# Attention phase: the order of GpSimd's late-modulation pieces and the place of their eviction

## The chip, the cores and the metric

The kernel runs on one core of a Trainium2 chip. The metric is the device time of one execution in microseconds (us). The time before is the median of three runs.

## What is computed

One layer of a hybrid diffusion model over 2048 latent tokens of width 1024 with 256 context tokens: a modulation, a mixer (a recurrent group and a windowed attention group), an output projection with a layer norm and a second modulation, and a mixture of experts. Cut to what matters here:

```
m_lat = silu_c @ w_mod[l] + b_mod[l]
sh1, sc1, g1, sh2, sc2, g2 = jnp.split(m_lat[:, None, :], 6, axis=-1)
h_lat = modulate(x, sh1, sc1)
# window_attention: scores over a band of 3*128 keys and 256 context keys, with a sink
p = jax.nn.softmax(jnp.concatenate([s_band, s_ctx, s_sink], -1), axis=-1)
# after the mixer
x = layer_norm(ALPHA * x + g1 * y_lat, ln1_g[l], ln1_b[l])
h_lat = modulate(x, sh2, sc2).reshape(B * S, D)
```

The second half of m_lat (sh2, sc2, g2; 3072 columns) isn't needed before the output projection. The kernel computes it beside attention: this is the "late modulation".

## The kernel before

The program is a row of phases, each a block in which every engine has its own instruction stream, and the next phase begins when all streams of the block have ended.

**Attention** (phase_attention) goes over 16 tiles of 128 queries, in 8 pairs (PAIRS), each tile with 8 heads (NH). For a head, TensorE makes the scores (L1099), VectorE takes the row minimum of the negated scores (L1157), ScalarE the exponent with its sum (L1190), TensorE transposes it (L1111), ScalarE copies the high half (L1199), VectorE makes the low half (L1163), and TensorE multiplies with the values (L1128 to L1130). The order is written out by hand in `pairs`; the first pair and the last stand outside the loop. Once in a tile comes the sink: GpSimd's `inverse` subtracts (L1045), ScalarE takes the exponent (exp_sink, L1207, between the exponent of head 7 and the copy of head 6), GpSimd adds (L1050) and inverts (L1055), and VectorE's `normalise` (L1175) scales the tile's result, which SP stores (L1021).

Between the inverses GpSimd works off two other things:
- The late modulation: for each of 8 slabs of w_mod (128 rows of 3072 columns, 1.5 MB), three pieces of 1024 columns: a multiplication with a column of c (L1069) and an addition to `late` (L1071). SP loads slabs 0 and 1 (L1013, `load_late`) behind w_out, its companions and a row of b_mod (L1008), and each further one when the pieces of the slab that it overwrites are done. The first piece of a slab waits for its load.
- A row of w_out is multiplied with g1 (L1080), once in a pair, and at the end gnc is scaled (L1081).

**Output** (phase_output): TensorE first sums `late` over the partitions into PSUM (L1596). ScalarE evicts these sums (L1517), SP stores them as rows (L1301), waits, and loads sh2 and sc2 back as broadcasts (L1304); VectorE adds 1 to sc2 (L1462) within its step for tile 0. ScalarE then makes the high halves of the 8 blocks of w_out (`high_w`, L1476), four before the first tile's `prepare` (L1482 to L1497) and four behind it; VectorE makes the low halves (L1368). TensorE's products of a tile need them. VectorE's long chain of the layer norm begins at L1401.

Of the kernel before, what the change touches and what calls it, by code (L numbers as in the profile page):

```python
# [12 lines left out]
ALU = mybir.AluOpType  # L13
ACT = mybir.ActivationFunctionType
# [3 lines left out]
D = 1024  # L18
KD = D // P
# [164 lines left out]
LATE_N = LATE_W // 8  # L184


def late_modulation(arena):

    return arena[:, 0:LATE_W]


OUT_W0 = 27000
# [722 lines left out]
def phase_attention(nc, env):  # L915
# [3 lines left out]
    g = env  # L919
    sem, arena, ps, ps_row, small, idn = g["sem"], g["arena"], g["ps"], g["ps_row"], g["small"], g["idn"]  # L920
# [17 lines left out]
    late_ld, late_ok, late_d = g["done"]["wmod_ld"][0:2], g["done"]["wmod_ld"][3], g["done"]["win_hi"]  # L938
    LATE_LD, LATE_OK, LATE_D = DONE["wmod_ld"], DONE["wmod_ld"], DONE["win_hi"]
    late = late_modulation(arena)  # L940
    slab = [arena[:, LATE_W * (j + 1):LATE_W * (j + 2)] for j in range(2)]
    assert 3 * LATE_W <= KT0
    LATE_P = LATE_W // D
# [4 lines left out]
    PAIRS = T_LAT // 2  # L948
# [39 lines left out]
    with nc.Block() as block:  # L988
# [47 lines left out]
        @block.gpsimd  # L1036
        def _(pool):

            def inverse(i, j):
                t = 2 * i + j  # L1040
                pool.wait_ge(s_min, START + NH * t + NH)
                pool.sem_inc(g["alone"], 1)
                pool.wait_ge(es_e, START + t)
                pool.sem_inc(g["alone"], 1)
                nc.gpsimd.tensor_tensor(es[j], nm[j], neg_sink, ALU.subtract).then_inc(es_d, 1)  # L1045
                pool.wait_ge(es_e, START + t + 1)
                pool.sem_inc(g["alone"], 1)
                pool.wait_ge(p_d, START + NH * t + NH)
                pool.sem_inc(g["alone"], 1)
                nc.gpsimd.tensor_tensor(es[j], den[j], es[j], ALU.add).then_inc(den_d, 1)  # L1050
                pool.wait_ge(den_d, START + 2 * t + 1)
                pool.sem_inc(g["alone"], 1)
                pool.wait_ge(o_d, START + t)
                pool.sem_inc(g["alone"], 1)
                nc.gpsimd.tensor_tensor(rd[j], es[j], minus, ALU.pow).then_inc(den_d, 1)  # L1055

            nc.gpsimd.memset(minus, -1.0).then_inc(w_gate, 1)
            pool.wait_ge(neg_ok, START + 1)
            pool.wait_ge(w_gate, START + 1)
            nc.gpsimd.memset(late, 0.0).then_inc(late_ok, 1)  # L1060

            def late_terms(k, lo, hi):
                if lo == 0:
                    pool.wait_ge(late_ld[k % 2], LATE_LD + 16 * (k // 2) + 16)
                    pool.wait_ge(late_ok, LATE_OK + 17)
                for n in range(lo, hi):
                    at = LATE_D + 2 * (LATE_P * k + n)
                    cols = slice(n * D, (n + 1) * D)
                    nc.gpsimd.tensor_scalar(slab[k % 2][:, cols], slab[k % 2][:, cols], g["c_col"][:, k:k + 1], None, ALU.mult)                        .then_inc(late_d, 1)  # L1069
                    pool.wait_ge(late_d, at + 1)  # L1070
                    nc.gpsimd.tensor_tensor(late[:, cols], late[:, cols], slab[k % 2][:, cols], ALU.add).then_inc(late_d, 1)  # L1071
            for i in range(PAIRS):
                inverse(i, 0)
                late_terms(i, 0, 2)
                inverse(i, 1)
                late_terms(i, 2, LATE_P)

                pool.wait_ge(w_ld, START + 16 * 7)
                row = arena[:, OUT_W0 + i * D:OUT_W0 + (i + 1) * D]
                nc.gpsimd.tensor_tensor(row, row, ow["g1"], ALU.mult).then_inc(w_gate, 1)  # L1080
            nc.gpsimd.tensor_scalar(ow["gnc"], ow["gnc"], W_SCALE, None, ALU.mult).then_inc(w_gate, 1)  # L1081

        @block.tensor
# [127 lines left out]
def phase_output(nc, env):  # L1211
# [3 lines left out]
    g = env  # L1215
    sem, arena, ps, ps_row, small, idn = g["sem"], g["arena"], g["ps"], g["ps_row"], g["small"], g["idn"]
    late = late_modulation(arena)
# [6 lines left out]
    late_rows = b["late_rows"].rearrange("p (i n) -> p i n", i=2)  # L1224
    late_mm, late_ev, late_st, late_ld = (g["done"][name] for name in ("mod_mm", "rows_done", "rows_st", "win_ld"))
    LATE_MM, LATE_EV, LATE_ST, LATE_LD = (DONE[name] for name in ("mod_mm", "rows_done", "rows_st", "win_ld"))
# [15 lines left out]
    sq, hi, lo, ssm, ss_d, ssv_d, pw_s = (sem("e_sq"), sem("e_hi"), sem("e_lo"), sem("e_ssm"), sem("e_ss"), sem("e_ssv"),  # L1242
                                              sem("e_pw_s"))
# [8 lines left out]
    def tiles(eng, first, step, finish):  # L1252

        first()
        step(0, 0)
        step(1, 1)
        with eng.Fori(1, T_LAT // 2 - 1) as i:
            step(2 * i, 0)
            step(2 * i + 1, 1)
        step(T_LAT - 2, 0)  # L1260
        step(T_LAT - 1, 1)
        finish()

    def known(t, low):

        return not isinstance(t, int) or t >= low

    def has_next(t):

        return not isinstance(t, int) or t + 1 < T_LAT  # L1270

    def half(t):

        return t // 2 if isinstance(t, int) else t >> 1
    with nc.Block() as block:
# [197 lines left out]
        @block.scalar  # L1473
        def _(act):
            def high_w(k):
                nc.scalar.activation(whi[:, k, :], wo[:, k, :], ACT.Copy, scale=b["gnc"][:, k:k + 1]).then_inc(w_hi, 1)  # L1476

            def prepare(t, j):
                act.wait_ge(in_ld[j], START + 32 * half(t) + 32)

                act.wait_ge(fold_d, START + 2 * t)
                nc.scalar.activation(b["ysq"], b[f"yT{j}"], ACT.Square).then_inc(sq, 1)  # L1482

                if known(t, 2):
                    act.wait_ge(o_y, START + t - 1)
                nc.scalar.activation(yhi[j], b[f"yT{j}"], ACT.Copy, scale=X_SCALE).then_inc(hi, 1)

                if known(t, 2):
                    act.wait_ge(ssv_d, START + t - 1)
                act.wait_ge(sq, START + 2 * t + 1)  # L1490
                nc.scalar.activation(b["asq"], b[f"at{j}"], ACT.Square, accum_out=ss[j][:, 1:2]).then_inc(sq, 1)
                act.wait_ge(a_tr, START + t + 1)
                if known(t, 2):
                    act.wait_ge(o_mm, START + t - 1)
                nc.scalar.activation(ahi[j], ps[:, 6, :], ACT.Copy, scale=X_SCALE).then_inc(hi, 1)
                act.wait_ge(ssm, START + t + 1)
                nc.scalar.activation(ss[j][:, 0:1], ps[:, 7, 64:65], ACT.Copy).then_inc(ss_d, 1)  # L1497

            def scaled(t, j):
                act.wait_ge(o_y, START + t + 1)  # L1500
                act.wait_ge(pw_s, START + t + 1)

                if known(t, 1):
                    act.wait_ge(v, START + NV * t - NV + 1)
                nc.scalar.activation(b["t0"], ps_row[:, 1024:2048], ACT.Copy, scale=sr[j][:, 0:1]).then_inc(o_act, 1)

            def route(t):
                for n in range(2):
                    act.wait_ge(h_tr, START + 2 * t + n + 1)

                    if n == 0:
                        act.wait_ge(r_mm, START + t)
                    nc.scalar.activation(b["h2T"][:, n * 512:(n + 1) * 512], ps[:, n, :], ACT.Copy).then_inc(h_ev, 1)

            def first():
                act.wait_ge(late_mm, LATE_MM + 1)
                nc.scalar.activation(late_rows, ps[:, 0:2, 0:LATE_N], ACT.Copy).then_inc(late_ev, 1)  # L1517
                for k in range(C_RNN):
                    high_w(k)
                prepare(0, 0)  # L1520
                for k in range(C_RNN, KD):
                    high_w(k)

            def step(t, j):
                if has_next(t):
                    prepare(t + 1, 1 - j)
                if known(t, 2):
                    route(t - 2)
                scaled(t, j)

            def finish():
                route(T_LAT - 2)
                route(T_LAT - 1)
            tiles(act, first, step, finish)

        @block.tensor
# [879 lines left out]
```

## Time and profile before

| | us |
|---|---|
| median of three runs | 2130.78 |
| lowest, highest | 2127.84, 2132.82 |
| profiled execution, its time | 2130.82 |
| its span, first to last instruction | 2129.0 |
| attention, from SP's first instruction to that of the output phase | 576.68 to 827.17 |

Times in the rows further down count from the start of this span. The name of an engine stands with the line of the kernel: L1207 ACT is the exponent of the sink. PE is TensorE, DVE VectorE, ACT ScalarE, POOL GpSimd, and SPq the DMA issues of SyncE. In a timeline each row has start, duration, engine, line and operation, and in brackets how long the engine sat idle before it and what ended this.

### The profile page before, as it was taken

To read this page: it belongs to the slowest core of one execution; us is meant where nothing else is said; L and a number is where in the kernel's file an instruction comes from. 1 tells how busy PE (TensorE), PEld (TensorE's weight loads), DVE (VectorE), ACT (ScalarE), POOL (GpSimd) and SP (SyncE) were. 2 spreads that over 40 slices of the span, in tenths; PEclk is the share of its full clock that TensorE was granted. 3 is DMA by queue.
4 is the path that set the end of the run, shared out by engine and by line. 5 is a ranking of instruction groups with operands and counts; after the bars stand their busy time and mean duration, and the time that the engine had idled before them with its cause. 6 is when DMAs were issued, how large, how long until landed. Compare 5 with 4: busy or idle time off the path is not lost. (4 is left out here: it accounts for less than half of the span.)

```text
span 2129.0 us, 41055 instructions
## 1 busy us (share of the span) xinstructions
PE 1782.7 (84%) x11690; PEld 1022.7 (48%) x11693; DVE 1496.2 (70%) x1855; ACT 1039.1 (49%) x1362; POOL 553.7 (26%) x456
## 2 busy tenths in 40 slices
PE   3488989799389996999914999999999889899947
PEld 0366666344177774555512454544444444444412
DVE  2576666488689996888978345666769888755537
ACT  2234243677378886333204134445556666534326
POOL 0000000000057785333313121223324323222213
PEclk9799999999799998999956999999999999999979
DMA  9321220565563322344336357886979999887537
GB/s 377 90 90 60 89 79 36 200 220 180 181 228 119 116 90 90 119 158 141 136 109 236 112 155 216 289 295 205 364 242 374 374 377 372 295 276 222 181 82 274
DMA packets 167790, 417.62 MB, mean 196 GB/s; under 512 B 16233, under 2 KB 24881, under 8 KB 166065
## 3 DMA queue, kind: packets, MB, share of 16 engines
q1 hardware_dynamic: 152898, 362.85, 46.8%
q0 software_dynamic: 14832, 54.01, 10.4%
q8 instruction: 33, 0.54, 0.1%
q14 instruction: 27, 0.22, 0.0%
HBM read 343.38 MB, written 73.44 MB: 196 GB/s over the span
## 5 line engine op out<-in xcount | busy, mean ns | idle before, releaser
L2060 DVE SCALAR_TENSOR_TENSOR arena<-arena 128x2048 f32 (+1 forms) x186 | 421.3, 2289 | 108.1 <-ACT arena L2004 50.9
L2140 PE MATMUL ps<-arena 128*128 x1200 | 458.3, 382 | 44.0 <-DVE arena L2060 43.8
L2141 PE MATMUL ps<-arena 128*128 x1200 | 458.1, 382 | 0.0
L2142 PE MATMUL ps<-arena 128*128 x1200 | 457.9, 382 | 0.0
L1998 ACT ACTIVATE arena<-arena 128x2048 f32 (+1 forms) x124 | 233.2, 1908 | 149.5 <-DMA arena<-w 62.3
L640 PE MATMUL ps<-arena 128*128 128x256 f16 (+1 forms) x1680 | 235.1, 301 | 21.1 <-DVE arena L525 21.1
L2140 PEld LDWEIGHTS ps<-arena 128*128 128x128 f16 x1200 | 118.0, 98 | 185.3 <-issue 59.0
L640 PEld LDWEIGHTS ps<-arena 128*128 128x128 f16 x1680 | 164.7, 99 | 85.7 <-DVE arena L525 15.2
L2142 PEld LDWEIGHTS ps<-arena 128*128 128x128 f16 x1200 | 118.1, 98 | 139.8 <-issue 3.4
L2141 PEld LDWEIGHTS ps<-arena 128*128 128x128 f16 x1200 | 117.9, 98 | 131.6 <-issue 3.5
L2004 ACT ACTIVATE arena<-arena 128x2048 f32 (+1 forms) x62 | 117.4, 1908 | 69.1 <-DMA arena<-w 52.6
L2060 DVE SCALAR_TENSOR_TENSOR arena<-ps,arena 128x512 f16<-128x512 f32 (+1 forms) x101 | 96.5, 955 | 68.9 <-ACT arena L2021 42.6
L1157 DVE CUSTOM_DVE_ANT_0 arena<-ps,arena,small 128x640 f32<-128x640 f32 x128 | 112.8, 881 | 16.5 <-issue 7.0
L1964 POOL COPY ix<-gidx 128x1 int32 (+1 forms) x50 | 26.0, 519 | 364.2 <-DVE arena L2097 364.2
L1099 PE MATMUL ps<-arena 128*128 (+3 forms) x768 | 93.0, 258 | 31.6 <-DMA arena<-qT_d 30.4
L2011 ACT ACTIVATE arena<-ps 128x1024 f16<-128x1024 f32 x51 | 52.0, 1020 | 122.8 <-PE ps L2135 122.8
L1111 PE MATMUL ps<-idn,arena 128*128 128x128 f32 x640 | 93.2, 276 | 20.5 <-ACT arena L1190 9.7
L1199 ACT ACTIVATE arena<-ps 128x640 f16<-128x640 f32 x128 | 90.1, 704 | 37.9 <-PE ps L1130 32.5
L1190 ACT ACTIVATE arena<-arena,small 128x640 f32<-128x640 f32 x128 | 105.0, 820 | 6.1 <-DVE small L1157 6.1
L1163 DVE SCALAR_TENSOR_TENSOR arena<-ps,arena 128x640 f16<-128x640 f32 x128 | 104.9, 819 | 3.1 <-ACT arena L1199 3.1
L2097 DVE SCALAR_TENSOR_TENSOR arena<-ps,gslot,arena 128x1024 f32<-128x1024 f32 x50 | 64.0, 1280 | 60.9 <-PE ps L2142 45.6
L1968 POOL DMA_INDIRECT x_d<-arena,ix x50 | 94.7, 1893 | 42.3 <-POOL ix L1964 38.5
(296 smaller groups left out, 3272.8 us busy)
## 6 DMA issues: line engine op xcount, KB each, us to landing
arena<-w SPq DMA_DIRECT2D x186, 1024.0 KB, 12.1
arena<-hT_d SPq DMA_DIRECT2D x64, 512.0 KB, 6.0
arena<-w_mod SPq DMA_DIRECT2D x16, 1536.0 KB, 8.0
h_d<-arena SPq DMA_DIRECT2D x17, 512.0 KB, 3.0
x_d<-arena SPq DMA_DIRECT2D x17, 512.0 KB, 2.6
arena<-x SPq DMA_DIRECT2D x8, 1024.0 KB, 6.4
hT_d<-arena SPq DMA_DIRECT2D x16, 512.0 KB, 3.1
arena<-x SPq DMA_DIRECT2D x16, 512.0 KB, 4.8
```

The lines of the kernel that those rows point to most:

```text
L640: mm = pe.matmul(o, lhs, rhs, start=first and n == 0, stop=last and n == 2)
L1111: mm = pe.transpose(pT(m)[:, q * P:(q + 1) * P], b[f"s{m % 4}"][:, q * P:(q + 1) * P], idn[:])
L1157: nc.vector.tensor_tensor_reduce(b[f"s{m % 4}"], scores_at(m), b[f"mask{j}"], -undo, neg_sink[:, h:h + 1], ALU.add, ALU.min, nm[j][:, h:h ...
L1163: nc.vector.scalar_tensor_tensor(b[f"plo{m % 2}"].bitcast(F16), pT(m), P_SCALE, b[f"phi{m % 2}"].bitcast(F16), ALU.mult, ALU.subtract).the ...
L1190: nc.scalar.activation(b[f"s{m % 4}"], b[f"s{m % 4}"], ACT.Exp, bias=nm[j][:, h:h + 1], scale=-1.0, accum_out=den[j][:, h:h + 1]).then_inc ...
L1968: pool.indirect_dma_start(g["x1_d"], bass.IndirectOffsetOnAxis(ix[:, 2:3], 0), b["y0"], None, compute_op=ALU.add)\
L1998: nc.scalar.activation(part(buf, whi, n * PIECE, PIECE), b["st"][:, n * PIECE:(n + 1) * PIECE], ACT.Copy, scale=W_SCALE).then_inc(hi13, 1)
L2004: nc.scalar.activation(part(buf, whi, n * PIECE, PIECE), b["st"][:, n * PIECE:(n + 1) * PIECE], ACT.Copy, scale=W_SCALE).then_inc(hi2, 1)
L2060: return nc.vector.scalar_tensor_tensor(dst, src, scale, high, ALU.mult, ALU.subtract)
L2140: pe.matmul(out, high, part(buf, whi, at, 512), start=first, stop=False)
L2141: pe.matmul(out, high, part(buf, wlo, at, 512), start=False, stop=False)
L2142: return pe.matmul(out, low, part(buf, whi, at, 512), start=False, stop=last)
```

## The change

GpSimd's stream in attention is put in another order. Before, for pair i: inverse of the even tile, pieces 0 and 1 of slab i, inverse of the odd tile, piece 2, gated row. After: pieces 0 and 1 of slab i, inverse of the even tile, piece 2, gated row, inverse of the odd tile. The scaling of gnc stays last. In the output phase, ScalarE's wait for TensorE's sums and their eviction move from the front of its stream to behind the first four `high_w` and the first tile's `prepare`. SP's, VectorE's and TensorE's streams aren't edited.

```diff
-            def late_terms(k, lo, hi):
-                if lo == 0:
+            def late_term(k, n):
+                if n == 0:
                     pool.wait_ge(late_ld[k % 2], LATE_LD + 16 * (k // 2) + 16)
                     pool.wait_ge(late_ok, LATE_OK + 17)
...
-            for i in range(PAIRS):
-                inverse(i, 0)
-                late_terms(i, 0, 2)
-                inverse(i, 1)
-                late_terms(i, 2, LATE_P)
+            def gated_row(k):
 
                 pool.wait_ge(w_ld, START + 16 * 7)
-                row = arena[:, OUT_W0 + i * D:OUT_W0 + (i + 1) * D]
+                row = arena[:, OUT_W0 + k * D:OUT_W0 + (k + 1) * D]
                 nc.gpsimd.tensor_tensor(row, row, ow["g1"], ALU.mult).then_inc(w_gate, 1)
+            for k in range(KD):
+                late_term(k, 0)
+                late_term(k, 1)
+                inverse(k, 0)
+                late_term(k, 2)
+                gated_row(k)
+                inverse(k, 1)
...
             def first():
-                act.wait_ge(late_mm, LATE_MM + 1)
-                nc.scalar.activation(late_rows, ps[:, 0:2, 0:LATE_N], ACT.Copy).then_inc(late_ev, 1)
                 for k in range(C_RNN):
                     high_w(k)
                 prepare(0, 0)
+                act.wait_ge(late_mm, LATE_MM + 1)
+                nc.scalar.activation(late_rows, ps[:, 0:2, 0:LATE_N], ACT.Copy).then_inc(late_ev, 1)
                 for k in range(C_RNN, KD):
                     high_w(k)
```

## Rows read from the trace of the kernel before

**Rows 1.** Busy time by stretch, middle of attention (columns named)
```profile
core 0: us, PE busy (x) PEld busy (x) DVE busy (x) ACT busy (x) POOL busy (x), PEclk, DMA share, GB/s
640.00:800.00 160.00, 146.58 (x2304) 124.66 (x2301) 149.07 (x277) 134.75 (x277) 121.47 (x72) 1.00 0.31 108
```

**Rows 2.** Groups by line, GpSimd: busy us, mean ns, then idle before
```profile
L1069 POOL TENSOR_SCALAR arena<-arena,c_col 128x1024 f32<-128x1024 f32 x24 | 68.4, 2852 | 5.0 <-DMA arena<-w_mod 5.0
```

**Rows 3.** Timeline of GpSimd, first and second tile of attention
```profile
603.78 2.86 POOL L1069 TENSOR_SCALAR arena<-arena,c_col 128x1024 f32<-128x1024 f32 x1 [5.05 <-DMA arena<-w_mod]
...
614.32 0.20 POOL L1045 TENSOR_TENSOR small<-small 128x8 f32<-128x8 f32 x1
```

**Rows 4.** Timeline of ScalarE: the sink's exponent of tiles 0, 1
```profile
596.14 0.20 ACT L1207 ACTIVATE small<-small 128x8 f32<-128x8 f32 x1
...
614.55 0.21 ACT L1207 ACTIVATE small<-small 128x8 f32<-128x8 f32 x1 [1.72 <-POOL small L1045]
```

**Rows 5.** Timeline of SP: the first two slabs of w_mod
```profile
594.10 2.26 SPq L1013 DMA_DIRECT2D arena<-w_mod  x2
```

**Rows 6.** Timeline of SP: mask loads at the ends of tiles 2, 3, 13
```profile
627.23 0.33 SPq L995 DMA_DIRECT2D arena<-masks  x1
...
641.51 0.33 SPq L995 DMA_DIRECT2D arena<-masks  x1
...
786.24 0.33 SPq L995 DMA_DIRECT2D arena<-masks  x1
```

**Rows 7.** Waits of 560 to 630 (us, times, longest), then those of L1157
```profile
PE ps L1099 <- DMA arena<-qT_d: 30.4, 2, 28.0
...
  POOL small L1045: 0.8, 5
```

**Rows 8.** Timeline of GpSimd and SP, end of attention; the store's landing time
```profile
815.50 0.21 POOL L1045 TENSOR_TENSOR small<-small 128x8 f32<-128x8 f32 x1
...
826.61 0.24 POOL L1081 TENSOR_SCALAR arena<-arena 128x8 f32<-128x8 f32 x1
821.14 0.32 SPq L1021 DMA_DIRECT2D attn_d<-arena  x1
827.17 0.37 SPq L1279 DMA_DIRECT2D arena<-yT_d  x1
...
DMA to landing us min/median/max: 2.0/2.0/2.0
```

**Rows 9.** Timeline, start of the output phase; landing of mod_rows' transfers
```profile
830.24 0.81 ACT L1517 ACTIVATE arena<-ps 128x768 f32<-128x768 f32 x1 [11.51 <-PE ps L1596]
830.95 4.25 ACT L1476 ACTIVATE arena<-arena 128x1024 f16<-128x1024 f32 x4
...
839.57 4.25 ACT L1476 ACTIVATE arena<-arena 128x1024 f16<-128x1024 f32 x4
...
831.08 2.46 SPq L1301 DMA_DIRECT2D mod_rows<-arena  x4
835.20 0.81 SPq L1304 DMA_DIRECT2D arena<-mod_rows  x2
...
DMA to landing us min/median/max: 4.0/4.9/15.1
...
846.73 0.68 DVE L1462 TENSOR_SCALAR arena<-arena 128x1024 f32<-128x1024 f32 x1
...
854.78 1.28 DVE L1401 SCALAR_TENSOR_TENSOR arena<-ps,small,arena 128x1024 f32<-128x1024 f32 x1 [6.14 <-PE ps L1569]
```

**Rows 10.** Busy time by stretch: TensorE's start and its pause
```profile
580.00:584.00 4.00, 2.81 (x16) 1.81 (x17) 0.89 (x2) 0.52 (x1) 1.16 (x1) 0.50 1.00 313
584.00:588.00 4.00, 3.26 (x29) 2.31 (x28) 2.89 (x7) 3.00 (x8) 0.00 (x0) 0.97 1.00 402
...
821.00:822.00 1.00, 0.00 (x0) 0.00 (x0) 0.05 (x1) 0.00 (x0) 0.92 (x1) 1.00 0.04 14
...
824.00:825.00 1.00, 0.00 (x0) 0.00 (x0) 0.00 (x0) 0.00 (x0) 1.00 (x2) 0.50 0.00 0
```

More of the change, by code:

```diff
@@ L1060, in _ @@
             nc.gpsimd.memset(late, 0.0).then_inc(late_ok, 1)
-            def late_terms(k, lo, hi):
-                if lo == 0:
+            def late_term(k, n):
+                if n == 0:
                     pool.wait_ge(late_ld[k % 2], LATE_LD + 16 * (k // 2) + 16)
                     pool.wait_ge(late_ok, LATE_OK + 17)
[L1066 to L1071, printed above, removed]
-            for i in range(PAIRS):
-                inverse(i, 0)
-                late_terms(i, 0, 2)
-                inverse(i, 1)
-                late_terms(i, 2, LATE_P)
+                at = LATE_D + 2 * (LATE_P * k + n)
+                cols = slice(n * D, (n + 1) * D)
+                nc.gpsimd.tensor_scalar(slab[k % 2][:, cols], slab[k % 2][:, cols], g["c_col"][:, k:k + 1], None, ALU.mult)\
+                    .then_inc(late_d, 1)
+                pool.wait_ge(late_d, at + 1)
+                nc.gpsimd.tensor_tensor(late[:, cols], late[:, cols], slab[k % 2][:, cols], ALU.add).then_inc(late_d, 1)
+            def gated_row(k):
                 pool.wait_ge(w_ld, START + 16 * 7)
-                row = arena[:, OUT_W0 + i * D:OUT_W0 + (i + 1) * D]
+                row = arena[:, OUT_W0 + k * D:OUT_W0 + (k + 1) * D]
                 nc.gpsimd.tensor_tensor(row, row, ow["g1"], ALU.mult).then_inc(w_gate, 1)
+            for k in range(KD):
[5 more added lines that the diff above has]
+                inverse(k, 1)
             nc.gpsimd.tensor_scalar(ow["gnc"], ow["gnc"], W_SCALE, None, ALU.mult).then_inc(w_gate, 1)
```

## The prediction

> **What bounds the kernel now.** I read the table of busy time by stretch first, over the middle of attention. In 160 us VectorE is busy for 149.07, TensorE for 146.58, ScalarE for 134.75 and GpSimd for 121.47 [rows 1]. So the attention loop is paced by the chain score, exponent, transpose, copy, low half, product, which runs through three nearly full engines. GpSimd isn't full. It is only a side branch, but one which ScalarE must wait for once in a tile: exp_sink (L1207) needs the subtraction at L1045, and ScalarE takes its instructions in order. While it stands there no further exponent and no further copy of a transposed tile is made, and so VectorE and TensorE stop after one or two more heads.
>
> Next I read the timeline of the two places that the change touches: the first tile and the border to the output phase. One piece of the late modulation is a multiplication (2852 ns on the mean [rows 2]) and a somewhat shorter addition on GpSimd. In the timeline two pieces last 614.32 - 603.78 = 10.54 us [rows 3].
>
> **Part 1: two pieces in front of the first tile.** In the kernel before, ScalarE's exp_sink of tile 0 ran at 596.14, without a wait [rows 4]. GpSimd began the first piece only at 603.78, after an idle stretch that the arrival of the first w_mod slab ended [rows 3]: SP had issued this load at 594.10 [rows 5], behind w_out, the broadcasts and the b_mod row. Nothing of the change touches that queue before this point, and GpSimd's instructions before it are the same too. So the slab lands at 603.78 again. But now GpSimd waits for it, and adds the two pieces, before the first inverse. The subtraction for tile 0 then starts at 614.32, which is just where before it started for tile 1 [rows 3], and exp_sink of tile 0 runs at 614.55 instead of 596.14: ScalarE is held for 18.41 us. That is the added wait. Behind it on ScalarE are the copy of head 6 and all exponents from head 8 on, and behind these VectorE's low halves, TensorE's products, and SP's store of tile 0.
>
> Not all of that is lost. In the kernel before, tile 1 was slow: its exp_sink also stood until 614.55, because GpSimd had started its two pieces late [rows 4], and TensorE's second wait for a q load was 30.4 - 28.0 = 2.4 us there [rows 7]. After the change that load is long in when ScalarE is released. So tile 1 after is released at 614.55, in the same way as tile 2 was before, and its minima should be complete where those of tile 2 were, at about 627.23; SP's mask loads mark these moments [rows 6]. Tile 2 after comes one odd-to-even step later. From the end of tile 3 to that of tile 13 are five pairs of tiles, (786.24 - 641.51) / 5 = 28.95 us each, and the even-to-odd step in a pair is 641.51 - 627.23 = 14.28 [rows 6], so the odd-to-even step is 14.67. From then on everything is one tile step late: **+14.7 us**. Bounds: 14.3 (the shorter step) below, and 18.4 above (if none of tile 1's slowness is given back).
>
> **Part 2: TensorE's clock.** In the stall TensorE has no work for some 16 us. The trace shows what that does: with TensorE idle at the end of attention, the granted clock was 1.00 at 821 to 822 and 0.50 (1.2 GHz) at 824 to 825 [rows 10]. When TensorE had begun attention it stood at 0.50 at 580 to 584, with 2.81 us of work, and at 0.97 on average at 584 to 588 [rows 10]. So the release at 614.55 restarts at 1.2 GHz for about 3.4 us. With TensorE over 91% busy in the loop [rows 1], half of that is lost: **+1.7 us**, an estimate. Bounds: 0 (the chain hides it) and 2.3 (4.6 us at the low clock, if the pauses between the heads keep it low longer). The Trainium skill, page "TensorE: Matmul & The Clock Gate", section "HAM oscillation — how this bites in real kernels", says the same of waits for data: the cold penalty is half of the throttled time. It speaks against this change, which opens such a pause; by a sum without this rule the forecast would be 1.7 lower.
>
> **Part 3: the steady loop.** The order in GpSimd's stream alternates as before (two pieces, inverse, one piece with a gated row, inverse), only the two pieces now stand in the odd-to-even gap, the longer one (14.67 against 14.28). In the kernel before, the last odd inverse started at 815.50 with no idle time in front of it [rows 8], about 1 us after the minima were there. But hardly anyone waited: VectorE's L1157 waited for it 0.8 us in all, in 5 places [rows 7]. I take **0**; bounds -0.8 and +0.5. SP's refill of a slab (L1013) waits for pieces that are now done earlier, so it is issued some us sooner, behind the store of the odd tile, in a stretch in which the DMA queues are mostly empty: 0.
>
> **Part 4: the end of attention.** In the kernel before, SP issued the last store at 821.14, which takes 2.0 us to land, so 823.1. The next phase began at 827.17 [rows 8], since GpSimd still had a piece, a gated row and the scaling of gnc (826.61 [rows 8]). After the change only the scaling is left behind the last inverse; it is done before the store. What is last now is the store: the phase begins at about 823.1 + 0.4 = 823.5 of the old time scale. **-3.7 us**; bounds -3.9 and -3.3.
>
> **Part 5: the eviction of the sums.** Before, ScalarE's first step in the output phase (the copy at L1517) waited for TensorE's sums until 830.24, and high_w began at 830.95 [rows 9], 3.78 us after the phase began at 827.17 [rows 8]. Now high_w starts at once, and everything up to the first tile's sums comes about 3.75 sooner. The first tile's loads don't stop that: they are issued in the same order, and ScalarE wants them only after four high_w of 4.25 us together [rows 9]. Then the copy stands in front of the second four high_w; its place in the line is 830.95 - 830.24 = 0.71. So high_w(4), 839.57 before [rows 9], comes 3.75 - 0.71 = **3.0 us** sooner, and with it TensorE's products and VectorE's first long chain (854.78 [rows 9]). Bounds: 0 and -3.75.
>
> What is late next: the rows. SP's four row stores, their wait and the two broadcasts stand behind the copy. Before, the stores were issued at 831.08, the broadcasts at 835.20 [rows 9], 4.1 later. After (in the old scale of the phase) the copy ends at about 836.6, the broadcasts are issued near 840.8 and land a median of 4.9 us later [rows 9], near 846. VectorE wants them at L1462, 846.73 before [rows 9], so 843.7 now: it stands for some 2.5 us. It has nothing on the path there until 854.78 - 3.0 = 851.8. That is its cover: 0. The refill for tile 2 (L1279 in SP's queue) stands behind the broadcasts too and now waits with them, to about 842. ScalarE wants it behind the second high_w (839.57 + 4.25 - 3.0 = 840.8) and the whole prepare of tile 1, which needs sums from GpSimd and TensorE; I count that as some 6 us more, near 847, and the refill as landed by then. Also 0, with little to spare.
>
> **The sum**, against the profiled execution (span 2129.0, its time 2130.82, practically the median of 2130.78): +14.7 + 1.7 + 0 - 3.7 - 3.0 = **+9.7 us**, so **2140.5 us**, slower by 0.45%. The phases behind (route, experts, combine) read what the output phase leaves and shift as a whole.
>
> **The rivals.**
> First, *the output phase gives nothing back*: the late rows or tile 2's refill hold VectorE or ScalarE long enough to eat part 5. Price 3.0: +12.7, 2143.5. It decides if the rows land after about 851. For it: two more queues now hang on the copy. Against it: 5 us of cover.
> Second, *the loop runs faster*: the lateness of GpSimd on odd tiles (about 1 us in each of 7 pairs) is on the path after all, and goes. Price -7: +2.7, 2133.5, within 0.2%. Against it: the 0.8 us of rows 7.
> Third, on the other side, *no stall at the first tile*: the wait that I see as 18.41 us would be covered, parts 1 and 2 fall away, and 4 and 5 remain: -6.7, 2124.1. It decides where slab 0 lands before 596.14 - 0.2 - 10.5 = 585.4, so that both pieces are done when exp_sink comes. For it: the end of attention is really freed. Against it: SP issues the load only at 594.10 [rows 5]. The change as a whole turns faster if the shift in attention is under 6.7 us.
>
> **How the numbers follow.** The forecast has 78 in 100, the first rival 10, the second 7, the third 5. A difference of 0.2% (4.3 us) is about what a measurement of this kernel can tell from no change; the three runs before spread from 2127.84 to 2132.82. Of the forecast's 78 I count 2 as ending within 0.2%. So slower 86, same 9, faster 5. The terms' bounds, not all at one end at once, and half of the spread of the runs give 2135.5 to 2144.5; this takes in the first rival, and leaves out the other two.
>
> **What will show it.** L1207's first wait: some 18 us on GpSimd's L1045 at 614.5 (part 1). SP's mask load for the second tile near 627 to 629, and 28.9 us for each pair from there. The granted clock at 0.50 around 614 to 618 (part 2). The output phase's first load about 0.4 us behind the landing of the last store (part 4), L1476 in its first tenth of a microsecond, and L1401's first start 24.6 us after the phase begins, against 854.78 - 827.17 = 27.6 before (part 5). Wrong it would be made by a slab that lands at another time, or by the cold restart being longer than one head or two.

## The result and the profile after

The changed kernel takes 2143.41 us (median of six runs, 2137.03 to 2145.09), against 2130.89 for the kernel before (six runs, 2127.84 to 2133.57): a ratio of 1.0056, 95% interval 1.004 to 1.0071. It is slower, by 12.5 us on the medians and 11.9 by the ratio (the ratio isn't simply that of the two medians, so the two readings differ a little in each run below). Measured again in another series (label a2_change_again, below) the ratio was 1.0039, interval 1.0027 to 1.0051, so 8.3 us, or 9.1 on the medians. The forecast was +9.7.

The profiled execution of the changed kernel has a span of 2135.2 us. Its attention begins at 577.18, 0.50 later than before (576.68), which is subtracted where positions are compared below. What changed lines are called now: the sink's exponent is L1211, the first late piece L1068, high_w L1480, the eviction L1524, VectorE's first long chain L1405.

First the timeline of ScalarE and of GpSimd at the first tiles; the rows of before that answer to them are [rows 3] and [rows 4].

```profile
596.32 0.82 ACT L1194 ACTIVATE arena<-arena,small 128x640 f32<-128x640 f32 x1
...
615.02 0.21 ACT L1211 ACTIVATE small<-small 128x8 f32<-128x8 f32 x1 [17.79 <-POOL small L1045]
...
630.79 0.20 ACT L1211 ACTIVATE small<-small 128x8 f32<-128x8 f32 x1
```

```profile
604.30 2.85 POOL L1068 TENSOR_SCALAR arena<-arena,c_col 128x1024 f32<-128x1024 f32 x1 [22.68 <-DMA arena<-w_mod]
607.24 2.34 POOL L1071 TENSOR_TENSOR arena<-arena 128x1024 f32<-128x1024 f32 x1
609.56 2.84 POOL L1068 TENSOR_SCALAR arena<-arena,c_col 128x1024 f32<-128x1024 f32 x1
612.48 2.34 POOL L1071 TENSOR_TENSOR arena<-arena 128x1024 f32<-128x1024 f32 x1
614.78 0.21 POOL L1045 TENSOR_TENSOR small<-small 128x8 f32<-128x8 f32 x1
```

ScalarE's last exponent of tile 0 begins at 596.32, and the sink's exponent at 615.02: 17.79 us of waiting for L1045. GpSimd's rows say where they come from. The slab lands at 604.30, 7.1 us after ScalarE became ready, and the two pieces last 10.5 us. In the whole attention this is the only wait of L1211.

Then TensorE in the stall, in the table of busy time by stretch (after the stretch: its length, busy time and count of PE, PEld, DVE, ACT and POOL, the granted clock, DMA share, GB/s). Before, all of these stretches stood at 1.00.

```profile
600.00:604.00 4.00, 0.00 (x0) 0.00 (x0) 0.00 (x0) 0.00 (x0) 0.00 (x0) 1.00 1.02 430
604.00:608.00 4.00, 0.00 (x0) 0.00 (x0) 0.00 (x0) 0.00 (x0) 3.62 (x2) 0.53 0.70 280
...
616.00:618.00 2.00, 1.18 (x7) 1.15 (x8) 2.00 (x4) 2.00 (x5) 2.00 (x2) 0.50 0.03 8
618.00:620.00 2.00, 2.00 (x24) 1.81 (x23) 0.90 (x2) 1.01 (x3) 2.00 (x1) 0.50 0.04 8
620.00:622.00 2.00, 2.00 (x26) 1.76 (x25) 0.44 (x3) 0.77 (x3) 1.92 (x2) 0.67 0.00 0
622.00:624.00 2.00, 0.88 (x11) 0.69 (x10) 2.00 (x5) 1.27 (x3) 2.00 (x2) 1.00 0.30 120
```

The clock falls to 0.50 while TensorE has nothing to do, and the first work behind the stall, from 616.8 to about 621.3, runs at the low clock, 1.2 GHz.

SP's mask loads mark the ends of tiles 1, 2, 3 and 13, the counterparts of [rows 6]:

```profile
629.04 0.33 SPq L995 DMA_DIRECT2D arena<-masks  x1
...
644.10 0.33 SPq L995 DMA_DIRECT2D arena<-masks  x1
...
658.50 0.33 SPq L995 DMA_DIRECT2D arena<-masks  x1
...
803.07 0.33 SPq L995 DMA_DIRECT2D arena<-masks  x1
```

Tile 1 now ends at 629.04, where before tile 2 ended at 627.23. A pair takes (803.07 - 658.50) / 5 = 28.91 us, against 28.95 before: the steady loop is untouched.

Last the border and the start of the output phase, on SP, ScalarE and VectorE, against [rows 8] and [rows 9]:

```profile
825.04 13.24 SPq L1021 DMA_DIRECT2D attn_d<-arena  x2
840.45 0.37 SPq L1283 DMA_DIRECT2D arena<-yT_d  x1
...
849.92 2.46 SPq L1305 DMA_DIRECT2D mod_rows<-arena  x4
853.49 0.81 SPq L1308 DMA_DIRECT2D arena<-mod_rows  x2
```

```profile
840.47 4.26 ACT L1480 ACTIVATE arena<-arena 128x1024 f16<-128x1024 f32 x4 [4.92 <-PEq L988]
...
849.09 0.81 ACT L1524 ACTIVATE arena<-ps 128x768 f32<-128x768 f32 x1
849.78 4.26 ACT L1480 ACTIVATE arena<-arena 128x1024 f16<-128x1024 f32 x4
...
860.73 0.63 ACT L1486 ACTIVATE arena<-arena 128x512 f32<-128x512 f32 x1 [0.16 <-DMA arena<-attn_d]
```

```profile
859.18 0.69 DVE L1466 TENSOR_SCALAR arena<-arena 128x1024 f32<-128x1024 f32 x1 [2.13 <-DMA arena<-mod_rows]
...
864.71 1.28 DVE L1405 SCALAR_TENSOR_TENSOR arena<-ps,small,arena 128x1024 f32<-128x1024 f32 x1 [4.64 <-PE ps L1573]
```

The last store is issued at 825.04 + 13.24 - 0.32 = 837.96, and the next phase begins 2.5 us later. High_w begins with the phase. VectorE stands for 2.13 us for the broadcasts, and then still 4.64 us for TensorE. Its first long chain starts 24.26 us behind the phase's start, against 27.61 before.

### The profile page after: what moved, and what is told of

Its sections match the earlier page's. It is cut to its first block and busy times, and to the rows that moved or that the text cites. A ratio compares the mean times of both kernels' runs of the same rounds, so it can differ in the third digit from the quotient of the medians.

```text
span 2135.2 us, 41055 instructions
## 1 busy us (share of the span) xinstructions
PE 1788.0 (84%) x11690; PEld 1025.5 (48%) x11693; DVE 1495.1 (70%) x1855; ACT 1039.2 (49%) x1362; POOL 550.7 (26%) x456
## 3 DMA queue, kind: packets, MB, share of 16 engines
q0 software_dynamic: 14832, 54.01, 10.4%
```

## The experiments

The time of a whole execution spreads by several microseconds even with the same kernel. The experts phase alone, which no edit touches, took 922.5 to 929.2 us in the traces (925.4 in the kernel before, 922.5 in the changed one). So besides the ratio each experiment is read by three stretches of its trace, with SP's first instruction of a phase as mark: *attention*; *start*, from the output phase's first instruction to VectorE's first long chain; and *both*, from attention's first instruction to the end of the output phase.

| kernel | ratio to before (95%) | attention | start | both |
|---|---|---|---|---|
| before | | 250.49 | 27.61 | 504.09 |
| the change | 1.0056 (1.004 to 1.0071) | 263.27 | 24.26 | 513.48 |
| a2_change_again | 1.0039 (1.0027 to 1.0051) | 262.27 | 24.27 | 512.53 |
| e1_order_alone | 1.0046 (1.0032 to 1.006) | 262.84 | 27.61 | 516.41 |
| e2_evict_alone | 0.998 (0.9969 to 0.9991) | 252.41 | 24.27 | 502.64 |
| e7_one_piece | 1.0012 (1.0 to 1.0023) | 258.61 | 24.27 | 508.83 |
| e6b_keep_warm_65 | 1.0035 (1.0025 to 1.0045) | 260.16 | 24.28 | 510.41 |
| e6_keep_warm | 1.0084 (1.007 to 1.0098) | 270.95 | 24.26 | 521.16 |
| e3_tail_only | 0.9969 (0.9958 to 0.998) | 246.26 | 25.96 | 498.19 |
| e4_gap0_light | 0.9951 (0.9936 to 0.9965) | 245.12 | 24.26 | 495.32 |
| e9_early_alone | 0.9991 (0.9981 to 1.0002) | 248.80 | 27.61 | 502.38 |
| e5_slab_early | 0.9949 (0.9935 to 0.9963) | 245.26 | 24.27 | 495.47 |
| e5b_slab_early_again | 0.9952 (0.9936 to 0.9968) | 244.93 | 25.95 | 496.81 |
| e8_tail_and_early | 0.9949 (0.9934 to 0.9963) | 244.15 | 25.95 | 496.04 |

**The two parts, each alone.** e1 takes the changed kernel and puts the eviction back; e2 takes the kernel before and moves the eviction alone.

```diff
 e1, against the changed kernel (e2: the other way round, against the kernel before)
             def first():
+                act.wait_ge(late_mm, LATE_MM + 1)
+                nc.scalar.activation(late_rows, ps[:, 0:2, 0:LATE_N], ACT.Copy).then_inc(late_ev, 1)
                 for k in range(C_RNN):
                     high_w(k)
                 prepare(0, 0)
-                act.wait_ge(late_mm, LATE_MM + 1)
-                nc.scalar.activation(late_rows, ps[:, 0:2, 0:LATE_N], ACT.Copy).then_inc(late_ev, 1)
```

> GpSimd's new order alone, the eviction stays at the front of ScalarE's stream. Theory A (stall at tile 0 of 18 us, of which one tile step and a cold restart stay, minus a free end of attention; the eviction is a term of its own): +14.7 + 1.7 - 3.7 = +12.7 us against before, so about 2143.5. The output phase begins about 12.8 us later than before and VectorE's first long chain again 27.6 us after it. Rival B (the two edits only pay together, since the eviction waits for sums that now come at once): the eviction at the front would cost nothing, so this kernel would be at the time of the full change, +9.4 in the trace up to the end of the output phase.

Measured: attention 12.35 us longer than before, start 27.61 to the hundredth, both +12.3. The eviction is a term of its own, as theory A has it, and rival B falls by the stretch: with the copy in front, the start takes 3.35 us more than in the change. The ratios can't show that: 1.0046 lies between the two measurements of the change.

> The eviction's move alone, GpSimd's order as before. Theory A: -3.0 to -3.4 us (first long chain of VectorE 24.3 us after the phase's start, against 27.6), so about 2127.6; attention unchanged, its last wait still GpSimd's tail. Rival C (the output phase gives it back behind the late rows): 0, 2130.9, with VectorE's first long chain again 27.6 us after the start or a longer wait later in the phase.

Measured: the start is 3.34 us shorter, and the ratio of 0.998 (-4.3 us, interval -6.6 to -1.9) is clear of 1. Rival C falls. Attention itself, with no edit in it, was 1.9 us longer than in the trace of before. Tile 1 did it: the sinks' exponents of tiles 0 and 1 stood at 600.14 and 618.43, 18.3 apart, nearly as before, but those of tiles 1 and 2 were 15.4 apart where before they were 14.1. So a single trace can differ by 1.9 us in attention with no edit there, and differences of that size between two traces, further down, prove little by themselves.

**The change again.**

> The changed kernel itself, once more, timed beside the kernel before on this chip. Theory A says +9.4 us to +9.8 (the shift of the marks up to the end of the output phase), so what the first measurement showed beyond that, +12.5, was spread between executions of the experts phase. Rival F says that about 3 us of it belong to the change, and come back here: +12.5.

Measured: 1.0039, and the stretch *both* +8.4 us. The interval, 5.8 to 10.9 us, leaves 12.5 out. Rival F falls: the 12.5 of the first measurement held some 3 us of spread.

**One piece in front of tile 0.** This measures what a microsecond of stall costs.

```diff
-            for k in range(KD):
-                late_term(k, 0)
-                late_term(k, 1)
-                inverse(k, 0)
-                late_term(k, 2)
-                gated_row(k)
-                inverse(k, 1)
+            late_term(0, 0)
+            pieces = iter([(k, n) for k in range(KD) for n in range(LATE_P)][1:])
+            rows = iter(range(KD))
+            for t in range(T_LAT):
+                inverse(t // 2, t % 2)
+                for _ in range([2, 2, 1, 2, 1, 2, 1, 2, 1, 2, 1, 2, 1, 2, 1, 0][t]):
+                    late_term(*next(pieces))
+                for _ in range([0, 0, 1, 0, 1, 0, 1, 0, 1, 0, 1, 0, 1, 0, 2, 0][t]):
+                    gated_row(next(rows))
```

> The change with one piece in place of two in front of tile 0; the second goes to the gap behind it, the gated rows to odd places further on. Theory A: the wait of the first sink's exponent falls by one piece, 5.3 us, to about 12.5, and all of it shows at the end: -5.3 against the change. With no piece there, the wait for the slab itself (7.7 of the 17.8 us) would go too. Rival H (a stall is given back in the loop, which has slack): the same end of attention as in the change.

The sink's exponent of tile 0, timeline of ScalarE in e7:

```profile
610.46 0.21 ACT L1213 ACTIVATE small<-small 128x8 f32<-128x8 f32 x1 [12.92 <-POOL small L1045]
626.43 0.19 ACT L1213 ACTIVATE small<-small 128x8 f32<-128x8 f32 x1
```

The wait fell from 17.79 (18.08 in the repeated trace) to 12.92, attention by 4.7 and 3.7 us against the two traces of the change, and the median beside a2 from 2141.92 to 2136.77, by 5.2. The stall is passed on about one to one; rival H falls.

**TensorE kept at work in the stall.** This takes away the cold restart (the first work behind the stall at the low clock) alone. The products go to a place in PSUM that is written anew later. e6b has 65 of them in place of 125.

```diff
             def transposes(i, m):
                 n = i * HEADS + m
+                if isinstance(n, int) and n == NH:
+                    for _ in range(125):
+                        pe.matmul(ps[:, 7, 384:512], idn[:], idn[:], start=True, stop=True)
```

> The full change, with 125 products of the identity on TensorE (into the place in PSUM of heads 6 and 7, which are written later) where it would stand idle in the stall of tile 0. Theory A: the granted clock stays at 1.00 through the stall, tile 1 ends 1.3 to 1.7 us sooner than in the changed kernel, total -1.5 against it. Rival E (the cold restart costs nothing on the path, tile 1's extra comes from the restart's latency): no gain in tile 1's end.

It ran into something else: each of these products is two passes of 0.112 us, so the stuffing lasted 28.1 us in place of the 14 that were meant, and TensorE itself became late (timeline of TensorE in e6):

```profile
600.50 28.08 PE L1112 MATMUL ps<-idn 128*128 128x128 f32 x250
628.41 0.71 PE L1119 MATMUL ps<-idn,arena 128*128 128x128 f32 x5
```

It says nothing on the clock's price. e6b has the right size.

> As e6_keep_warm with 65 products in place of 125. In e6 the 250 passes took 28.1 us and outlasted the stall by 12 us, which was not meant; 130 passes take 14.6 us and end about 1.5 us ahead of ScalarE's release. Theory A: clock 1.00 all through, tile 1 (from the first sink's exponent to the second) in about 14.1 us where the change needed 15.8, so -1.7 against the change. Rival E (the cold restart is off the path): 15.8 again.

Timeline of ScalarE in e6b, and one row of its busy time by stretch:

```profile
614.77 0.21 ACT L1215 ACTIVATE small<-small 128x8 f32<-128x8 f32 x1 [16.62 <-POOL small L1045]
628.41 0.20 ACT L1215 ACTIVATE small<-small 128x8 f32<-128x8 f32 x1
```

```profile
616.00:618.00 2.00, 1.43 (x25) 1.43 (x26) 1.96 (x4) 1.94 (x6) 2.00 (x2) 1.00 0.06 16
```

The clock stays at 1.00 all through the stall. The same five transposes are TensorE's first work behind it in both kernels (timeline of TensorE, first the change, then e6b):

```profile
616.82 1.30 PE L1115 MATMUL ps<-idn,arena 128*128 128x128 f32 x5 [17.41 <-DVE arena L1167]
```

```profile
616.57 0.74 PE L1119 MATMUL ps<-idn,arena 128*128 128x128 f32 x5 [1.73 <-DVE arena L1171]
```

From the first sink's exponent to the second it takes 13.64 us. The change took 15.77, its repetition 14.96 (611.98 to 626.94), e1 15.33 (611.84 to 627.17). So the cold restart costs 1.3 to 2.1 us, 1.7 on the mean of three, and rival E falls. The other traces agree: e7, which restarts at 0.50 too, took 15.97, and e5 and e5b (below), whose clock stays at 1.00 behind a short stall, took 13.80 each. In the whole time it can't be told apart: 2141.37 against 2141.92 for a2.

**The free end without the stall.** e3 leaves the front of tile 0 alone and spreads the pieces so that nothing lies behind the last inverse. e4 also makes the first gap light.

```diff
 the loop over k of the changed kernel becomes
+            pieces = iter([(k, n) for k in range(KD) for n in range(LATE_P)])
+            rows = iter(range(KD))
+            for t in range(T_LAT):
+                inverse(t // 2, t % 2)
+                for _ in range(ROWS[t]):
+                    gated_row(next(rows))
+                for _ in range(PIECES[t]):
+                    late_term(*next(pieces))
 e3: PIECES = [2, 1] * 6 + [2, 2, 2, 0];     ROWS = [0, 1] * 4 + [0, 2, 0, 2] + [0] * 4
 e4: PIECES = [1, 2] + [2, 1] * 5 + [2, 2, 2, 0]
     ROWS = [2, 0, 0, 2, 0, 1, 0, 1, 0, 1, 0, 1, 0, 0, 0, 0]
```

> The eviction moved as in the change, but nothing in front of tile 0: GpSimd's gaps 0 to 11 hold 2, 1, 2, 1, ... pieces as in the kernel before, gaps 12 to 14 two each, gap 15 (behind the last inverse) none, the gated rows in the odd gaps up to 11. Theory A: the stall was the price of moving the two pieces to the front, and the free end doesn't need it: -3.7 - 3.3 = -7.0 us against before, 2124; no wait over 3 us of the sink's exponent. Rival G (the loop had no room for the extra pieces: gaps of 10.5 us beside an inverse of 3.9 in a step of 14.3 to 14.7): waits of the sink's exponent in tiles 12 to 15, and more than 2128.

Measured: 0.9969, 6.6 us faster by the ratio and 5.2 on the medians, where 7.0 was expected; attention 4.2 us shorter, and no wait of the sink's exponent but the 2.18 us of tile 1 that the kernel before has too. So rival G falls. The start took 25.96 in place of 24.3, which is told in the last section.

> As e3_tail_only, but the gap behind tile 0 holds two gated rows and one piece in place of two pieces, so that GpSimd is done with them before tile 1 ends although the slab lands late. Theory A: the wait of tile 1's sink (2.2 us in e3) is gone, about -1 to -2 against e3, near -8 against before; the query load that comes late behind the slabs stays. Rival K (that wait was hidden behind the query load anyway): the same as e3.

The timeline of GpSimd and of ScalarE in e4:

```profile
603.51 4.68 POOL L1077 TENSOR_TENSOR arena<-arena 128x1024 f32<-128x1024 f32 x2
608.27 2.85 POOL L1068 TENSOR_SCALAR arena<-arena,c_col 128x1024 f32<-128x1024 f32 x1
```

```profile
600.95 0.20 ACT L1212 ACTIVATE small<-small 128x8 f32<-128x8 f32 x1
...
615.56 0.20 ACT L1212 ACTIVATE small<-small 128x8 f32<-128x8 f32 x1
```

GpSimd fills the time until the slab lands with gated rows, whose data are there. Tile 1's sink doesn't wait any more. The two exponents are 14.6 us apart (18.4 before), of which 1.4 is only that the first came later behind the start of attention; the second came 2.4 us sooner. The ratio is 0.9951: 10.4 us faster than before by the ratio, 8.8 on the medians and by the stretch. Rival K says that this is the same as e3. That isn't settled: attention is 1.1 us shorter than in e3, less than the 1.9 by which e2's trace differed without an edit, and the intervals of the two ratios overlap.

**The slab earlier.** e5 is the full change with another order in SP's queue. e9 is the kernel before with that order alone, e8 is e3 with it.

```diff
             for j in range(2):
                 load(0, j)
 
+            sp.dma_start(slab[0], g["w_mod"][0:P, FRONT:6 * D]).then_inc(late_ld[0], 16)
+            sp.wait_ge(late_ok, LATE_OK + 1)
+            sp.dma_start(late[0:1, :], g["b_mod"][0:1, FRONT:6 * D]).then_inc(late_ok, 16)
             sp.dma_start(wo, g["w_out"].rearrange("(k p) n -> p k n", p=P)).then_inc(w_ld, 16)
...
-            sp.wait_ge(late_ok, LATE_OK + 1)
-            sp.dma_start(late[0:1, :], g["b_mod"][0:1, FRONT:6 * D]).then_inc(late_ok, 16)
...
-            for k in range(2):
-                load_late(k)
+            load_late(1)
```

> The full change, but SP loads slab 0 and the row of b_mod in front of w_out instead of behind it (and slab 1 alone where both stood). Theory A (the stall is the wait for slab 0 plus two pieces, nothing else): the slab lands near 585, both pieces are done near 595.5 to 597, the wait of the first sink's exponent falls from 17.8 us to 0 to 2, the clock stays high, and the whole is -3.7 (free end) - 3.3 (eviction) and up to 3 us of tile 1's slowness before: 2121 to 2125. Rival D (two pieces in front of the inverse hold the first tile by themselves, or the queries of tile 0 come late behind the slab, or w_out comes late for the gated row): more than 5 us of stall stay somewhere in the first two tiles, over 2128.

The timeline of GpSimd and of ScalarE in e5:

```profile
589.19 2.86 POOL L1067 TENSOR_SCALAR arena<-arena,c_col 128x1024 f32<-128x1024 f32 x1 [6.61 <-DMA arena<-b_mod]
```

```profile
599.95 0.21 ACT L1210 ACTIVATE small<-small 128x8 f32<-128x8 f32 x1 [1.22 <-POOL small L1044]
613.75 0.20 ACT L1210 ACTIVATE small<-small 128x8 f32<-128x8 f32 x1
```

The stall shrank to 1.22 us (1.91 in e5b), although both pieces still stand in front of tile 0, and a kernel that was slower by 0.4% to 0.6% became faster by 0.5%. The moment of landing was what decided; rival D falls. The load that GpSimd waited for last was now the row of b_mod, which e5 moves together with the slab, so the two loads aren't told apart. The repetition gave the same (0.9952).

> e5_slab_early once more, so that the three others have it beside them on the same chip: -10 us against before (its marks gave -8.6 up to the end of the output phase).

> The kernel before with SP's order of e5_slab_early alone: GpSimd's order and the eviction as before. Theory A: it takes away tile 1's slowness (18.4 us where 14 is the step), which came from late arrivals: -2 to -4, and nothing else, since the end of attention is GpSimd's tail as before. It says how much of e5's gain is the early slab by itself: the rest is the change, with its stall taken away (about -7). Rival J (the queue's new order costs elsewhere, w_out for the rows or the masks and queries of tile 2): 0 or slower.

Measured: 0.9991, no difference that can be told; by the stretches -1.7 us, all in attention, where -2 to -4 was expected. Tile 1 takes 15.5 us there (600.15 to 615.66 between the exponents) in place of 18.4, and no sink waits. But 1.7 us is no more than e2's trace differed without an edit, so rival J (nothing gained) stays open. Taken as they stand, the traces put about 1.7 of e5's -8.6 us down to the early slab by itself, and 6.9 to what the change gives once its stall is gone, close to the 3.7 + 3.3 of its two gains.

> GpSimd's order of e3_tail_only (nothing in front of tile 0, nothing behind the last inverse) and SP's order of e5_slab_early (slab 0 and the row of b_mod in front of w_out). Theory A: with the slab early, the order in front of tile 0 matters for no more than the 1.2 us that ScalarE still waited in e5: -1.2 against e5. Rival I: the gaps of 2 pieces in the shorter steps cost as much as they did in the kernel before (waits at tile 1), so the same as e5 or slower.

Measured: attention is the shortest of all, 244.15, by 0.8 and 1.1 us against e5b and e5; the ratio is that of e5, 0.9949. That is near the expected 1.2, but within what one trace differs from another, and the times show nothing of it. Rival I (the same as e5) isn't excluded.

## Why the prediction was right

**Part 1, the stall.** Expected 18.41 us on ScalarE, with tile 1 then ending where tile 2 ended before, and +14.7 behind it. Seen: a wait of 17.79, and tile 1's end at 629.04 - 0.50 = 628.54 against 627.23, so 1.3 later than the bare shift by a tile; the cold restart stands for that. At the last sink's exponent the two terms together are (833.29 - 577.18) - (816.46 - 576.68) = 16.3 us, against 14.7 + 1.7 = 16.4. The traces of a2 and e1 give 15.3 and 15.9, so that it fits to a tenth is luck. e5 and e7 show the cause: e7 that the stall is paid one to one, e5 that it is the slab's landing.

**Part 2, the clock.** Expected +1.7, between 0 and 2.3, from a low clock of 3.4 us of which half is lost. e6b gives 1.3 to 2.1. The size is right partly by luck: the low clock lasted longer, about 4.5 us (616.8 to 621.3), near the 4.6 of the upper bound, and less than half of it showed in the time. The Trainium skill, page "TensorE: Matmul & The Clock Gate", section "HAM oscillation — how this bites in real kernels", puts the cold penalty at half of the throttled time, and this case agrees with it nearly: half of 4.5 us is 2.2, just above what e6b shows.

**Part 3, the loop.** 28.91 us for a pair against 28.95: 0, as taken. The second rival (7 us back from GpSimd's lateness on odd tiles) is out: nothing came back.

**Part 4, the end.** Expected -3.7. Attention as a whole grew by 263.27 - 250.49 = 12.8 us, and 16.3 - 12.8 = 3.5. The phase began 2.5 us behind the last store's issue, against 2.4 expected. The experiments bear it out: from the last sink's exponent to the next phase it is 10.7 us in the three traces with GpSimd's old order at the end (before, e2, e9) and 7.1 to 7.2 in all eleven others.

**Part 5, the eviction.** Expected -3.0; it was -3.35 in the change, -3.34 in its repetition and in e2 alone. The second high_w stands at 849.78, 9.33 behind the phase's start, where before it was 12.40, so 3.07 sooner as predicted. The 0.28 more came between there and VectorE's chain, in a step that the prediction has no term for: the last addition of GpSimd's fold, for which TensorE waits before tile 1's products. First before, then after:

```profile
846.98 0.75 POOL L1349 TENSOR_TENSOR arena<-arena 128x128 f32<-128x128 f32 x1 [0.18 <-POOL arena L1346]
```

```profile
857.21 0.46 POOL L1353 TENSOR_TENSOR arena<-arena 128x128 f32<-128x128 f32 x1 [0.18 <-POOL arena L1350]
```

It took 0.75 or 0.76 us in the three traces with the eviction in front (before, e1, e9), and 0.46 in the eleven others. In the kernel before, VectorE is at work on its addition of 1 to sc2 (846.73 to 847.41) beside it; in the change, VectorE stands and waits for the broadcasts. That this is the cause wasn't tested. The covers held, narrowly: VectorE waited 2.13 us for the broadcasts (2.5 expected), with 4.64 us of idle time left behind it, and ScalarE waited 0.16 us for the refill of tile 2, where I had said "little to spare". So the first rival is out too.

**The sum.** +9.7 expected, +9.4 in the stretch that holds both edits (513.48 - 504.09), +8.4 in the repeated trace; +11.9 and +8.3 by the ratios of the two timings (+12.5 and +9.1 on the medians), whose intervals (8.5 to 15.1, and 5.8 to 10.9) both hold it. All five terms were seen near their size, so the mechanism was right; that the total came within 0.3 of the first trace is partly luck, since the second stands 0.9 lower. The third rival, no stall, didn't happen, but its condition was the right one: e5 fulfils it nearly and turns the sign.

**A version that beats both.** e4, e5 and e8 are all 0.4% to 0.5% faster than the kernel before (2123.85, 2122.91, 2123.53 us, against 2132.64, 2132.95 and 2132.64 beside them). Their intervals overlap, so none is shown to be the best. e4 needs no change of SP's queue.

## What to carry to other kernels

Side work on a helper engine is free in the gaps of the main chain, but at the first gap it also waits for its data, and what stands behind it in that engine's stream waits along: look up when the load lands, add the work, and compare with the moment at which the main chain wants the helper. Emptying the end of a phase and keeping its front free don't exclude each other if the gaps between have room. And fill the wait for data with work whose data are there, as e4 does.

## What the runs showed of the hardware

The start of the output phase took 24.26 to 24.28 us with the moved eviction in eight traces, and 25.95 or 25.96 in three (e3, e5b, e8), with nothing between. e5 and e5b are the same kernel. The table of busy time by stretch shows the difference, first in e5:

```profile
842.00:844.00 2.00, 2.00 (x11) 0.93 (x10) 0.76 (x2) 1.61 (x3) 0.71 (x1) 1.00 1.05 318
844.00:846.00 2.00, 2.00 (x11) 0.88 (x10) 0.00 (x0) 1.21 (x4) 1.19 (x2) 1.00 0.06 17
```

and here in e5b, whose phase begins 4.4 us later in its span:

```profile
842.00:844.00 2.00, 0.31 (x2) 0.00 (x0) 2.00 (x3) 1.47 (x4) 1.87 (x1) 1.00 0.95 225
844.00:846.00 2.00, 0.99 (x6) 0.63 (x7) 0.34 (x1) 0.17 (x1) 0.78 (x2) 1.00 1.00 375
846.00:848.00 2.00, 2.00 (x8) 0.69 (x7) 0.86 (x2) 1.07 (x2) 0.56 (x1) 0.60 1.12 348
848.00:850.00 2.00, 2.00 (x7) 0.75 (x6) 0.00 (x0) 1.71 (x5) 1.12 (x3) 0.54 0.28 85
```

Between tile 0's products and tile 1's, TensorE pauses for GpSimd's fold, with 2.34 us of idle time in e5 and 2.71 in e5b. In e5 the clock stays at 1.00 behind it; in e5b it falls to about 0.5 after TensorE has already begun again, and 11 products in two microseconds become 7. The price is 1.7 us. So behind a pause as short as this the clock fell in three traces and stayed up in eight, with the same code in one pair of them. The three in which it fell are those with the longest pauses: 3.04, 2.71 and 2.65 us of idle time (e3, e5b, e8), against 1.62 to 2.57 in the eight. TensorE begins again at the same place in all eleven, 17.3 us behind the phase's start. The pause is longer where the clock rose sooner within tile 0's products, which then ended sooner: in e5b it was up 11.8 us behind the phase's start, in e5 12.6. That is an order seen in eleven traces of one program, and no run tests it. With the eviction in front (before, e1, e9) the start was 27.61 in all three traces.
